# Issuing the query and value weight loads one projection chunk further back in SyncE's queue

## The reference

```python
mod = silu(c) @ w_ada + b_ada                 # 1024 x 6144: shift1, scale1, gate1, shift2, scale2, gate2
h = rms_norm(x, norm1_g) * (1 + scale1) + shift1
z = h @ w_in                                  # x_lru 512, g_lru 512, q_lat 256, kv_lat 128, k_rope 32
# recurrent group: causal conv of x_lru -> gates r, i -> scan h = a*h + u -> * gelu(g_lru)
q = rms_norm(q_lat, q_lora_norm_g) @ w_uq     # 256 x 768, then norms per head and a rotation
kv = kv_lat @ w_ukv                           # 128 x 1024: keys and values of 8 heads
attn = attend(q, kv, k_rope, caches)          # prompt: causal; samples: paged cache of 4096 + 1
x = x + gate1 * (concat(norm(lru), norm(attn)) @ w_o)
x = x + gate2 * (conv-gated MLP of the modulated norm of x)
```

## Time and profile before

| what | value |
|---|---|
| median of 3 runs | 1013.28 us (1012.67 to 1016.78) |
| the profiled execution's own time | 1014.83 us |
| its span, first to last instruction | 1013.0 us |
| TensorE (PE) busy | 944.9 us, 93% |
| VectorE (DVE) busy | 659.4 us, 65% |
| ScalarE (ACT) busy | 528.5 us, 52% |
| GpSimd (POOL) busy | 183.0 us, 18% |
| moved by DMA | 100.13 MB |
| mean granted TensorE clock | 0.961 of full |

### The profile page before, as it was taken

The page is one execution under the profiler, slowest core; times in us unless marked ns, Lnnn a source line. Parts: engine busy times, 40 slices in busy tenths (PEclk is TensorE's granted clock), DMA queues, the critical chain, the costliest instruction groups (busy, mean ns, idle before and its releaser), DMA issues.

```text
span 1013.0 us, 20471 instructions
## 1 busy us (share of the span) xinstructions
PE 944.9 (93%) x7908; PEld 880.4 (87%) x7908; DVE 659.4 (65%) x1259; ACT 528.5 (52%) x1183; POOL 183.0 (18%) x186
## 2 busy tenths in 40 slices
PE   6599798889999999999988988999999999999997
PEld 3388675679999999999987988999999999999997
DVE  2694267538889879879783557777777777732321
ACT  2323553458898898988973333444434443321210
POOL 0021120322333343333210131000101001000000
PEclk9699899879999999999996998999999999999999
DMA  9965740600122022022101430333333331653202
GB/s 339 333 193 170 229 160 7 231 1 2 28 100 84 22 104 85 22 85 93 55 19 45 134 69 27 99 83 83 83 106 101 83 83 41 171 154 79 61 4 85
DMA packets 106289, 100.13 MB, mean 99 GB/s; under 512 B 7119, under 2 KB 94943, under 8 KB 104126
## 3 DMA queue, kind: packets, MB, share of 16 engines
q1 hardware_dynamic: 102422, 77.91, 26.4%
q0 software_dynamic: 3456, 20.97, 5.9%
q10 hardware_dynamic: 340, 0.27, 0.1%
HBM read 96.41 MB, written 2.94 MB: 98 GB/s over the span
## 4 chain that ended last, share of the span: by engine, by line
PE 85%; DVE 7%; ACT 3%; DMA 3%; issue 1%; SPq 0%; DVEq 0%; ACTq 0%
PE ps L874 50%; PE ps L1242 19%; PE ps L869 7%; DMA RW<-w_ada 3%; PE ps L900 2%; PE ps L1149 2%; PE ps L1200 1%; PE ps L1237 1%; PE ps L1175 1%; PE ps L1035 1%; DVE RB L1913 1%; DVE normed_low L1814 1%; DVE RB L1788 0%; DVE RB L2235 0%; PE ps L1100 0%
## 5 line engine op out<-in xcount | busy, mean ns | idle before, releaser
L874 PE MATMUL ps<-normed_high,up_weights_high 128*128 128x260 f32 x704 | 142.7, 284 | 3.4 <-DVE normed_low L1814 3.2
L874 PE MATMUL ps<-normed_high,up_weights_low 128*128 128x260 f32 x704 | 142.3, 284 | 0.0
L874 PE MATMUL ps<-normed_low,up_weights_high 128*128 128x260 f32 x704 | 142.1, 284 | 0.0
L1654 ACT ACTIVATE up_weights_high<-RW 128x1024 fp32r<-128x1024 f32 x44 | 46.6, 1061 | 137.2 <-PE ps L874 133.3
L1242 PE MATMUL ps<-key_weights_high,latents_high 128*128 128x260 f32 x528 | 117.4, 304 | 0.7 <-ACT RB L1596 0.6
L832 POOL TENSOR_TENSOR latents_low<-RB,latents_high 128x512 fp32r<-128x512 f32 (+1 forms) x72 | 86.2, 1198 | 174.8 <-ACT latents_high L1549 174.8
L874 PEld LDWEIGHTS ps<-normed_high,up_weights_high 128*128 128x128 f32 x704 | 109.2, 190 | 4.1 <-issue 3.3
L874 PEld LDWEIGHTS ps<-normed_high,up_weights_low 128*128 128x128 f32 x704 | 109.0, 189 | 0.0
L874 PEld LDWEIGHTS ps<-normed_low,up_weights_high 128*128 128x128 f32 x704 | 108.8, 189 | 0.0
L1242 PE MATMUL ps<-key_weights_low,latents_high 128*128 128x260 f32 x528 | 107.2, 285 | 0.0
L1242 PE MATMUL ps<-key_weights_high,latents_low 128*128 128x260 f32 x528 | 107.2, 285 | 0.0
(11 more groups left out here) (314 smaller groups left out, 2178.2 us busy)
## 6 DMA issues: line engine op xcount, KB each, us to landing
RW<-w_ada SPq DMA_DIRECT2D x24, 1024.0 KB, 8.6
RW<-w_up SPq DMA_DIRECT2D x44, 512.0 KB, 5.0
RW<-w_down SPq DMA_DIRECT2D x8, 1408.0 KB, 7.2
RW<-w_in SPq DMA_DIRECT2D x11, 512.0 KB, 8.0
RB<-w_o SPq DMA_DIRECT2D x8, 512.0 KB, 4.1
RB<-x_prompt SPq DMA_DIRECT2D x2, 1024.0 KB, 12.6
o_y_p<-RB SPq DMA_DIRECT2D x4, 512.0 KB
cst<-consts SPq DMA_DIRECT2D x1, 845.0 KB, 11.2
```

The lines of the kernel that those rows point to most:

```text
L874: last = mm(ps[j % 4][rows[0]:rows[1], h, 0:H], lhsT, src[:, h * H:(h + 1) * H], start=start, stop=stop)
L1654: A(wuH[:, KT * g:KT * g + KT, :], wup[:, c, KT * g:KT * g + KT, :], ACT.Copy).then_inc(s_whi, 1)
```

## The change

In SyncE's loop the call of `query_weights()` moves from the pass n = 8 to the pass n = 9: from behind `later_modulation(8)` to behind `later_modulation(9)`. `w_in(9)` and `later_modulation(9)`, which came after it, now come before it. Nothing else changes, on no other engine either.

```diff
                 w_in(n)
                 for c in chunks:
                     later_modulation(c)
-                if n == 8:
+                if n == 9:
                     query_weights()
```

## The result

The changed kernel took a median of 1006.5 us (1006.09 to 1007.54, 4 runs) against 1014.15 us (1012.67 to 1016.78, 4 runs) of the kernel before: ratio 0.9923, 95% interval 0.99 to 0.9947, so some 7.8 us or 0.8% faster. The profiled execution's own time is 1007.54 us, its span 1005.7.

The account below looks back on a forecast made before the run. The prediction took TensorE's own sequence to bound the kernel, stalled at L900 for modulation chunk 9. Savings of 6.85 (wait), 0.87 and 1.24 (clock) sum to 8.96 us, so 1013.28 - 8.96 = 1004.3 us; range 1001.5 to 1007.8.

Parts of the forecast that it names:

- The wait: At L900, TensorE's 6.85 us wait for modulation chunk 9 goes, because that chunk is issued at 94.6 instead of 107.51.
- The clock term of 2.11: Chunk 9 and the norm sum behind it run at the upper clock level, saving 0.87 and 1.24 us; bounds 0 and 2.11.
- the sum: Whole saving on TensorE's chain: 6.85 + 0.87 + 1.24 = 8.96 us, with nothing on the other side.
- What is late next: Chunk 10 lands at about 117.0, wanted by TensorE at 118.96: 2.0 us in hand, the thinnest margin.
- Rival (b): The wait moves to chunk 10, landing 2.4 us late at 121.4: gain 6.5, time 1006.8 us; chance 0.17.
- the one uncertain term: Later lowered-clock stretches (154.1 to 158.5, 196.0 to 207.5) may fall elsewhere: up to 5.3 us either way, taken as 0.
- rival (a): The clock falls anyway, or what it gave back is paid elsewhere: gain only the bare wait, 1006.4 us; chance 0.12.

Follow-up runs that it names:

- e2: Kernel before with only modulation chunk 9 moved ahead of the query and value weight loads, w_in(9) left behind them; ratio to before 0.9922.
- e3: Kernel before with only w_in(9) moved ahead of the query and value weight loads, modulation chunk 9 left behind them; ratio to before 0.9993.
- e8: Changed kernel with three more loads, 1.01 MB, between the query and value weights, ahead of chunk 10; ratio to before 0.9916, median 1004.94 us.
- e1: Changed kernel run once more, unaltered, for a second trace; ratio to before 0.9917.
- e9: Changed kernel with TensorE made to wait before chunk 9 for the squares of the key/value latent, 2.72 us; ratio to before 0.9952, median 1009.53 us.
- e4: Changed kernel with the query and value weight loads one pass further back, behind w_in(10) and chunks 10 and 11; ratio to before 0.9915.
- e6: Changed kernel with TensorE made to wait before chunk 9 for ScalarE's high part of w_in(8), 3.66 us; ratio to before 0.9989, median 1013.44 us.
- e7: Changed kernel with TensorE made to wait before chunk 9 for GpSimd's low part of w_in(8), 6.09 us; ratio to before 1.0, median 1013.86 us.

## Why the prediction was right, and where it was off

**The wait.** Right in every step: w_in(9) at 91.07 (said 91.2), chunk 9 at 94.50 (94.6) and landed 5.1 us later (5.2), the barrier unmoved at 105.61 (105.8), the wait of 6.85 gone. e2 and e3 show that it was chunk 9's place in the queue that made the wait, and not w_in(9)'s.

**The clock term of 2.11.** Chunk 9 and the norm sum run at the upper level, as said. Stretch one gives 44.67 - 35.80 = 8.87 against the 8.96 of the sum. Since the wait is 6.85, the clock's part is 2.02, as chunk 9 and the norm sum lay inside the spell (114.4 to 121.2).

**What is late next.** Chunk 10 landed at 110.43 + 7.1 = 117.5 (said 117.0) and was used at 118.88 (118.96): 1.4 us in hand instead of 2.0. Rival (b) did not happen; e8 shows that it was near. The Trainium skill ("DMA: Bandwidth & Descriptors", "Queues, rings and completion order"), by which loads of one issuing engine need not complete in order, had spoken for it. Chunk 10 landed 0.5 us later than my sum said, not the 4.4 of this rival; no row shows whether interleaving made the 0.5.

**The step that was off** is the one uncertain term, "if these fall elsewhere ... I take 0". It measured +1.3 to +1.8 us in three traces against three: a spell at the lower clock now covers part of w_in(11) or more of the L1035 block at the restart. This is rival (a) in its second wording, "what it gave back is paid elsewhere", beside a wait that went as forecast. So the first half of (a), the clock falling anyway at chunk 9, is wrong and the second came true in part: 8.87 less 1.3 to 1.8 is 7.1 to 7.6 in the traces, against the 7.8 of the ratio, and (a) had 6.85.

I had called this term scatter, on the word of the Trainium skill ("TensorE: Matmul & The Clock Gate", "What's actually happening"), that the moment of the change differs from run to run. The traces agree as to the place of the spell, which differs between e1 and the other two of the changed kernel. As to its cost they speak for a loss: stretch two of the kernel before repeated within 0.1 us in three traces, that of the changed kernel within 0.35. But six traces are not all runs. The three of the kernel before had a mean granted clock of 0.961 or 0.962, while its 51 timings beside the experiments have 0.954 to 0.967, and their spans lie 5.5 us apart, more than the 3.3 by which the start moved in any trace; so stretch two very likely varies more than 0.1 us. Over all 57 timings of the kernel before and ten of the changed one the means are 1014.7 and 1006.5. That is 8.1 us (95% interval about 7.5 to 8.7) against 8.8 in stretch one, averaged over the three traces of before. So on average some 0.6 us, and hardly more than 1.2, is lost outside stretch one. The term is a small cost on average; the 1.3 to 1.8 us of the traces is not shown to hold for every run.

**The number.** 1004.3 was worked out from a median of 1013.28 of three runs. With the fourth it is 1014.15, and 1014.5 to 1014.7 in the 15 to 19 runs beside the experiments. Of the 2.2 us between 1004.3 and 1006.5, 0.9 is this base. The 1.3 left has the size of the term above, though with four runs on each side it could as well be chance in part.

**What stays open** is what fixes the place of the spell. That the order of loads alone fixes it is not so: e8 has the changed order and 859.11 in stretch two, e9 with its pause 858.94, while e2, e3, e4, e6 and e7 have 859.9 to 860.3, and three of them (e3, e6, e7) stop TensorE before chunk 9, as the kernel before does. A shift of where TensorE stops by some fraction of a microsecond may decide; this is a guess, as no run was made that shifts it alone.

## What to carry to other kernels

When a queue's head waits for a semaphore, ask of every load behind it whether it waits for anything itself, and by when it is wanted. One that is wanted first and free to go belongs ahead of the barrier, and the load that the barrier is for can go back as long as its own use lies well behind its landing in a crowded queue (9 us here, not the 5 of an empty one). And price a stall of TensorE as the wait plus half of the slow spell that is left when it restarts: shortening a stall by 2.0 us that still let the clock fall returned 1.4 in stretch one (0.7 by the ratio of the whole kernel, within the noise), removing it returned the whole 8.9 there and 7.8 to 8.4 in the whole kernel.

## What the runs showed of the hardware that was not expected

In stretch one, by one trace each, a stop of 2.7 us costs 1.75 us of clock beyond itself and one of 3.7 us costs 2.98, more than the 1.7 to 2.1 of the stop of 6.9 us. The granted clock fell 2.6 to 4.0 us after TensorE had stopped (2.6 in e6 and e9, 4.0 in e7, 3.1 to 4.0 in the traces of before), so a stop of one length can cost differently from run to run; the ten runs of e6 reach from 1010.28 to 1014.5 us. In e9 the engine had just restarted, at 113.68, when the granted clock was down to 0.50 for the whole of the next microsecond, and it was back from 117 on:

```profile
113.00:114.00 1.00, 0.32 (x4) 0.20 (x8) 0.75 (x1) 1.00 (x2) 0.00 (x0) 0.79 0.86 295
114.00:115.00 1.00, 1.00 (x16) 0.38 (x8) 0.00 (x0) 0.98 (x2) 0.35 (x1) 0.50 0.93 336
...
116.00:117.00 1.00, 1.00 (x3) 0.72 (x3) 0.00 (x0) 0.00 (x0) 1.00 (x1) 0.50 0.78 143
117.00:118.00 1.00, 1.00 (x7) 0.88 (x5) 0.00 (x0) 0.00 (x0) 0.00 (x0) 1.00 0.64 164
```

So the loss in stretch one is far from proportional to the wait: 4.5, 6.6, 7.5, 8.5 and 8.9 us for waits of 2.7, 3.7, 4.9, 6.1 and 6.9. The last 3.2 us of waiting cost 2.2, the first 2.7 cost 4.5. By the medians of the whole kernel the losses are 3.1, 7.0, 7.6, 7.5 and 8.2: there the short pause is cheaper, and from 3.7 us of waiting on the loss grows little.
